# Attention with compressed, selected and local keys: two heads side by side on 64-row tiles, and the compressed keys of four tiles and two heads as one unit

## The chip, the core and the metric

The kernel runs on one core of one Trainium2 chip. The metric is device microseconds for one execution. TensorE (PE) does the matrix products, VectorE (DVE) and ScalarE (ACT) the elementwise work, GpSimd (POOL) some fills, and SyncE (SP) issues most transfers. Everything here is in 4-byte floats.

## The reference

Two transformer blocks run one after the other on 512 tokens of width 1024. The change is in the mixer of the second block, in the attention of its first eight heads. Each query head has 64 dimensions; four query heads share one of two key and value heads. Every query looks at three sets of keys, each with a softmax of its own, and the three results are added with one gate each:

```python
m_c = cmp_end[None, :] <= tpos[:, None]
s_c = jnp.einsum('bkgqd,bknd->bkgqn', qq, k_cmp) * scale      # 31 compressed keys
p_c = masked_softmax(s_c, m_c) * m_c
o_c = jnp.einsum('bkgqn,bknd->bkgqd', p_c.astype(v_cmp.dtype), v_cmp)
...                                                            # o_s: keys of selected blocks
...                                                            # o_w: keys of a local window
return gg[..., 0:1] * o_c + gg[..., 1:2] * o_s + gg[..., 2:3] * o_w
```

With 512 tokens there are 8 blocks of 64 keys and 16 may be selected, and the window is 512 long: selected and local keys are both all causal keys, each with its own keys and values. The second eight heads ("forgetting" attention) add a term from cumulated forget gates to the logits and are not in the change, though they run through one of the functions that it touches.

## The kernel before

Each engine has its own instruction stream, written as a list of phases; semaphores order the engines against each other. Tokens come in four tiles of 128. The eight heads are handled as four pairs: pair i holds one head of each key head, so a 128-partition column of queries holds two heads in rows 0 to 63 and 64 to 127. Four banks of PSUM take logits, two take turned probabilities, two take sums. The order of tiles is (2, 3, 1, 0), so a unit of tile q is q + 1 key blocks of 128 wide.

`grouped_attention` (L2422) goes through `attend` (L1498). For each pair a loop turn has 24 units: 2 heads, 4 tiles, 3 key sets. The compressed set is one unit of 128 columns (31 keys and padding) per head and tile. `copy_queries` (L2412) first copies each head's queries to a buffer whose other 64 rows are zero, so each logits product uses all 128 rows and a single head. A unit goes through: logits on PE (L1546); mask and row minimum on DVE (L1587); exponential with row sum on ACT (L1566); reciprocal (L1592) and a diagonal matrix with reciprocal times gate (L1597) on DVE; then PE multiplies each block of the probabilities with that diagonal, which turns and scales it in one (L1545); ACT copies the result out (L1571); PE sums with the values (L1553). The turn ends with ACT's copy of the pair's sums (L1575). At its start the turn waits for the work of the turn before.

`paired_attention` (L1610) is used for the first block's attention (name `dsa`) and for the forgetting attention (`fox`). It is written out without a loop. A unit is two heads of one tile. The logits of head 0 come from rows 0 to 63 and those of head 1 from rows 64 to 127 of the array (L1649), into two banks. DVE masks both heads (L1727), ACT takes both exponentials (L1698), DVE scales the probabilities in place (L1741, L1744), PE turns them with transposes (L1671), ACT copies both heads at once (L1708), and PE sums head 0 into columns 0 to 63 and head 1 into columns 64 to 127 (L1684). In step t the engines take these up in this order:

```python
# PE:  logits(t), turn(t - 2), sums(t - 3)
# ACT: exponentials(t), copy(t - 2)
# DVE: mask and minimum(t), scaling(t - 1)
```

turn(n) waits for scaling(n) and copy(n - 1), sums(n) for copy(n), logits(t) for the masking of unit t - 2. `fox` units have one more product per head, from the forget sums (L1652). `dsa` pairs also make their keys and values on the way (L2004 to L2020).

Of the kernel before, what the change touches and what calls it, by code (L numbers as in the profile page):

```python
# [23 lines left out]
NCMP = 31  # L24
CMP_L = 32
# [9 lines left out]
def columns(*parts):  # L35

    at, out = 0, {}
    for name, width in parts:
# [10 lines left out]
CB = columns(("causal", T), ("cos", T), ("sin", T), ("rot", P), ("twice0", P), ("twice1", P), ("cmp_mask", QT * P),  # L49
             ("cmp_valid", QT))  # L50
# [50 lines left out]
def build(nc, d):  # L101

    ctx = ExitStack()
    with ctx:
# [1393 lines left out]
        def attend(name, scope, turns, work, out, ready, before, zero_first=()):  # L1498


            N = len(work)
            sx = keep(f"{name}_masked", [P, 4, T], scope)
            probs = keep(f"{name}_probs", [P, 4, T], scope)
            probsT = keep(f"{name}_probsT", [P, 2, T], scope)
            diag = keep(f"{name}_diag", [P, 4, P], scope)
            stat = keep(f"{name}_stat", [P, 3, 4], scope)
            MAX, SUM, INV = range(3)
            L, TR, O = 0, 4, 6
            order = []
            for t in range(N + 4):  # L1510
                order += [("L", t)] * (t < N) + [("T", t - 3)] * (3 <= t < N + 3) + [("O", t - 4)] * (t >= 4)
            a_order = []
            for t in range(N + 3):
                a_order += [("exp", t)] * (t < N) + [("PT", t - 3)] * (t >= 3)
            d_order = []
            for t in range(N + 1):
                d_order += [("max", t)] * (t < N) + [("inv", t - 1), ("diag", t - 1)] * (t >= 1)

            def names(eng, seq):
                return before[eng][0] + [f"{a}{n}" for a, n in seq]  # L1520
            S = {"pe": steps(f"{name}_pe", names("pe", order)), "act": steps(f"{name}_act", names("act", a_order) + ["out"]),
                 "dve": steps(f"{name}_dve", names("dve", d_order))}

            def earlier(what, n, back, turn):

                who = S[{"max": "dve", "T": "pe", "PT": "act", "O": "pe"}[what]]
                return who(f"{what}{n - back}", turn) if n >= back else who(f"{what}{N + n - back}", turn, 1)

            def pe(pe):
                S["pe"].enter(pe)  # L1530
                for r in ready:
                    pe.wait_ge(*reached(*r))
                with pe.Fori(0, turns) as i:
                    before["pe"][1](pe, i, S)
                    for what, n in order:
                        w = work[n]
                        if what == "L":
                            pe.wait_ge(*earlier("max", n, 4, i))
                            out_l = ps[:, L + n % 4, 0:w["w"]]
                            ins = mm(out_l, w["query"], w["keys"])  # L1540
                        elif what == "T":
                            pe.wait_ge(*S["dve"](f"diag{n}", i))
                            pe.wait_ge(*earlier("PT", n, 2, i))
                            for b in range(w["w"] // P):
                                ins = mm(ps[:, TR + n % 2, b * P:(b + 1) * P], probs[:, n % 4, b * P:(b + 1) * P], diag[:, n % 4, :])  # L1545
                        else:  # L1546
                            pe.wait_ge(*S["act"](f"PT{n}", i))
                            if n == 0:
                                pe.wait_ge(*S["act"]("out", i, 1))
                            hh, q = w["head"], w["tile"]  # L1550
                            nb = w["w"] // P
                            for b in range(nb):
                                ins = mm(ps[hh * HD:(hh + 1) * HD, O, q * P:(q + 1) * P], w["values"][b],  # L1553
                                         probsT[:, n % 2, b * P:(b + 1) * P], w["first"] and b == 0, w["last"] and b == nb - 1)
                        ins.then_inc(*S["pe"].step(f"{what}{n}"))

            def act(act):
                S["act"].enter(act)
                with act.Fori(0, turns) as i:
                    before["act"][1](act, i, S)  # L1560
                    for what, n in a_order:
                        w = work[n]["w"]
                        if what == "exp":
                            act.wait_ge(*S["dve"](f"max{n}", i))
                            act.wait_ge(*earlier("T", n, 4, i))
                            ins = nc.scalar.activation(probs[:, n % 4, 0:w], sx[:, n % 4, 0:w], ACT.Exp, scale=-1.0,  # L1566
                                                       bias=stat[:, MAX, n % 4:n % 4 + 1], accum_out=stat[:, SUM, n % 4:n % 4 + 1])
                        else:
# [487 lines left out]
        def mixer_inputs(scope, h, branch):  # L2056
# [54 lines left out]
            def pool(pool):  # L2111
                pool.wait_ge(*reached(*branch[0]))
                for n in (kcmp, vcmp):
                    nc.gpsimd.memset(n[:, :], 0.0).then_inc(zeroed, 1)
# [827 lines left out]
```

## Time and profile before

| | |
|---|---|
| median of 3 runs | 3237.2 us (3234.42 to 3240.36) |
| the profiled execution | 3233.23 us |
| its span in the profile | 3231.4 us |
| the changed attention, from the last head input to the first product of `fox` | 2477.1 to 2657.5 us |
| `fox`, four pairs | 2657.5 to 2705.9 us |

The span is from the first to the last instruction. Times inside the profile are microseconds from its start. PE, DVE and ACT shares of a window say how busy an engine was; "PEld" is the load of the array's stationary operand, which overlaps products. A 4-byte product shows as two records, a transpose as one. PEclk is the granted clock of TensorE as a share of 2.4 GHz.

### The profile page before, as it was taken

Reading aid. Unit: us, or ns where it says so; the run is one execution under the profiler, and the core shown is the slowest. Engines: PE = TensorE matmul, PEld = TensorE weight load, DVE = VectorE, ACT = ScalarE, POOL = GpSimd, SP = SyncE. Lnnn points to the kernel's source line nnn. Section 1 sums busy time; section 2 is a strip of 40 time slices with the busy share of each in tenths; the row PEclk is TensorE's granted clock in tenths of the full one; section 3 lists DMA queues with packets and bytes.
Section 4 is the critical chain, followed back from the end, with each engine's and each line's share of the span. In section 5 each row is a group of like instructions: output and inputs, shape, how many; then the busy total and the mean of one; then the engine's idle time right before and its main releaser. Section 6 shows DMA issues by size and latency. Waiting matters only on the chain.

```text
span 3231.4 us, 49675 instructions
## 1 busy us (share of the span) xinstructions
PE 2942.0 (91%) x19222; PEld 2146.1 (66%) x19222; DVE 1448.2 (45%) x2408; ACT 1060.4 (33%) x1648; POOL 231.5 (7%) x221
## 2 busy tenths in 40 slices
PE   4998999888999899879999799999898997899998
PEld 1566666637888644558888488886655665688885
DVE  6466555624333327654333443332335555533335
ACT  1323222214432222634431344311112555344214
POOL 1122222201000101300000000000001000000000
PEclk9999999999999989999999899999798998999999
DMA  4223222222222111022222123221120000222312
GB/s 185 89 90 112 103 103 102 94 104 78 104 96 108 61 40 65 1 78 80 102 101 107 40 78 104 101 98 68 54 83 33 1 0 14 91 104 91 115 54 98
DMA packets 45837, 260.85 MB, mean 81 GB/s; under 512 B 4952, under 2 KB 7400, under 8 KB 26888
## 3 DMA queue, kind: packets, MB, share of 16 engines
q1 hardware_dynamic: 45128, 254.33, 22.2%
q10 hardware_dynamic: 576, 4.57, 0.4%
q8 instruction: 105, 1.72, 0.2%
q14 instruction: 28, 0.23, 0.0%
HBM read 256.73 MB, written 2.15 MB: 80 GB/s over the span
## 4 chain that ended last, share of the span: by engine, by line
PE 83%; DVE 7%; issue 3%; ACT 3%; DMA 2%; POOL 1%; PEld 1%; DVEq 0%; SPq 0%; ACTq 0%; POOLq 0%; PEldq 0%
PE psum L191 82%; DMA weights<-in_ada 1%; DVE weights L227 1%; PEld psum L191 1%; PE psum L1671 1%; DVE ln_rstd L1134 0%; DVE attention_in L1727 0%; POOL join L507 0%; POOL join L496 0%; POOL XT_pairs L500 0%; ACT dsa_probs L1698 0%; DVE rms_rstd L1214 0%; DVE dsa_probs L1744 0%; DVE group_norm L765 0%; DVE ff_weights_lo L1246 0%
## 5 line engine op out<-in xcount | busy, mean ns | idle before, releaser
L1246 DVE TENSOR_TENSOR ff_weights_lo<-weights,ff_weights_hi 128x1024 fp32r<-128x1024 f32 (+1 forms) x120 | 159.7, 1332 | 328.6 <-ACT ff_weights_hi L1243 328.6
L1246 DVE TENSOR_TENSOR ffn_weights_lo<-weights,ffn_weights_hi 128x1024 fp32r<-128x1024 f32 (+1 forms) x120 | 159.7, 1332 | 322.0 <-ACT ffn_weights_hi L1243 322.0
L191 PE MATMUL psum<-ff_in_hi,ff_weights_hi 128*128 128x512 f32 x704 | 276.2, 392 | 21.0 <-DVE ff_in_lo L1143 17.6
L191 PE MATMUL psum<-ffn_in_hi,ffn_weights_hi 128*128 128x512 f32 x704 | 276.0, 392 | 17.9 <-DVE ffn_in_lo L1222 14.4
L1243 ACT ACTIVATE ffn_weights_hi<-weights 128x1024 fp32r<-128x1024 f32 (+1 forms) x120 | 137.4, 1147 | 448.1 <-PE psum L191 448.1
L1243 ACT ACTIVATE ff_weights_hi<-weights 128x1024 fp32r<-128x1024 f32 (+1 forms) x120 | 137.4, 1147 | 445.1 <-PE psum L191 445.1
L191 PE MATMUL psum<-ffn_in_lo,ffn_weights_hi 128*128 128x512 f32 x704 | 275.5, 391 | 0.0
L191 PE MATMUL psum<-ff_in_hi,ff_weights_lo 128*128 128x512 f32 x704 | 275.4, 391 | 0.0
L191 PE MATMUL psum<-ff_in_lo,ff_weights_hi 128*128 128x512 f32 x704 | 275.3, 391 | 0.0
L191 PE MATMUL psum<-ffn_in_hi,ffn_weights_lo 128*128 128x512 f32 x704 | 275.1, 391 | 0.0
L191 PEld LDWEIGHTS psum<-ff_in_hi,ff_weights_hi 128*128 128x128 f32 x704 | 133.2, 189 | 51.4 <-issue 19.2
L191 PEld LDWEIGHTS psum<-ffn_in_hi,ffn_weights_hi 128*128 128x128 f32 x704 | 133.1, 189 | 48.3 <-issue 16.0
L191 PEld LDWEIGHTS psum<-ffn_in_hi,ffn_weights_lo 128*128 128x128 f32 x704 | 133.1, 189 | 27.8
L191 PEld LDWEIGHTS psum<-ff_in_lo,ff_weights_hi 128*128 128x128 f32 x704 | 133.3, 189 | 27.6
L191 PEld LDWEIGHTS psum<-ff_in_hi,ff_weights_lo 128*128 128x128 f32 x704 | 133.0, 189 | 27.9
L191 PEld LDWEIGHTS psum<-ffn_in_lo,ffn_weights_hi 128*128 128x128 f32 x704 | 133.1, 189 | 27.5
L191 PE MATMUL psum<-ff_hidden_hi,ff_weights_hi 128*128 128x512 f32 x352 | 136.9, 389 | 0.0
L191 PE MATMUL psum<-ff_hidden_lo,ff_weights_hi 128*128 128x512 f32 x352 | 136.9, 389 | 0.0
L191 PE MATMUL psum<-ffn_hidden_hi,ffn_weights_hi 128*128 128x512 f32 x352 | 136.9, 389 | 0.0
L191 PE MATMUL psum<-ffn_hidden_lo,ffn_weights_hi 128*128 128x512 f32 x352 | 136.9, 389 | 0.0
L191 PE MATMUL psum<-ff_hidden_hi,ff_weights_lo 128*128 128x512 f32 x352 | 136.9, 389 | 0.0
L191 PE MATMUL psum<-ffn_hidden_hi,ffn_weights_lo 128*128 128x512 f32 x352 | 136.9, 389 | 0.0
(452 smaller groups left out, 5383.4 us busy)
## 6 DMA issues: line engine op xcount, KB each, us to landing
weights<-in_ada SPq DMA_DIRECT2D x96, 512.0 KB, 4.3
weights<-in_ff_in SPq DMA_DIRECT2D x44, 1024.0 KB, 4.7
weights<-in_ffn_in SPq DMA_DIRECT2D x44, 1024.0 KB, 4.7
weights<-in_ff_out SPq DMA_DIRECT2D x16, 1408.0 KB, 6.0
weights<-in_ffn_out SPq DMA_DIRECT2D x16, 1408.0 KB, 6.0
weights<-in_rwkv SPq DMA_DIRECT2D x8, 1792.0 KB, 8.0
weights<-in_fox_qkv SPq DMA_DIRECT2D x4, 1536.0 KB, 6.7
residual<-in_x ACTq DMA_DIRECT2D x2, 2048.0 KB, 10.7
```

Source lines behind the costliest of these rows:

```text
L191: return nc.tensor.matmul(out, lhsT, rhs, start=start, stop=stop)
L227: return nc.vector.tensor_tensor_reduce(ada_tile(n), ada_tile(n), cond, scale=1.0, scalar=0.0, op0=ALU.mult, op1=ALU.add, accum_out=inner[ ...
L1243: return nc.scalar.activation(sp_.hi[u][:, 0:width], slot[s][:, u * width:(u + 1) * width], ACT.Copy)
L1246: return nc.vector.tensor_tensor(sp_.lo[u][:, 0:width], slot[s][:, u * width:(u + 1) * width], sp_.hi[u][:, 0:width].bitcast(F32), ALU.sub ...
L1671: ins = nc.tensor.transpose(ps[:, TR + hh, blk], probs[:, n % 3, hh, blk], ident)
```

## The change

`attend` and `pair_queries` are removed. `grouped_attention` now builds units for `paired_attention`: per pair eight units of two heads (four tiles, selected and local keys) and one "blocks" unit that holds the compressed keys of all four tiles and both heads in 256 columns, 32 for each tile and head. The compressed values of the two key heads lie in partitions 0 to 30 and 32 to 62 now, in their own columns. Gates go into the scaling of the probabilities. The sums of tile q start with the compressed part, then selected, then local keys. The fill of zeros around the queries and their copies go; the mask table of the compressed keys shrinks from 512 to 256 columns. `fox` now waits for the first of two conditions only, which is the last copy of sums.

```diff
-        def attend(name, scope, turns, work, out, ready, before, zero_first=()):
...
+                        if "blocks" in u:
+                            for q in range(QT):
+                                for hh in range(2):
+                                    ins = mm(ps[:, 2 * (t % 2) + hh, q * NB:(q + 1) * NB], u["query"][hh][:, q * P:(q + 1) * P], u["keys"][hh])
+                        for hh in range(0 if "blocks" in u else 2):
                             ins = mm(ps[:, 2 * (t % 2) + hh, 0:u["w"]], u["query"][hh], u["keys"][hh], True, "extra" not in u)
...
+                        if "blocks" in units[n]:
+                            for q in range(QT):
+                                ins = mm(ps[0:2 * NB, TR, q * P:(q + 1) * P], probs[:, n % 3, 0, q * 2 * NB:(q + 1) * 2 * NB], ident)
...
+                        if "blocks_at" in u:
+                            q = u["blocks_at"]
+                            for hh in range(2):
+                                rows = slice(hh * NB, (hh + 1) * NB)
+                                ins = mm(ps[hh * HD:(hh + 1) * HD, O + u["pair"] % 2, q * P:(q + 1) * P], small.values[rows, hh * HD:(hh + 1) * HD],
+                                         small.probsT[rows, u["pair"] % 2, q * P:(q + 1) * P], True, False)
...
+                        if "blocks" in units[t]:
+                            act.wait_ge(masked, 2 * (n0 + t) + 2)
+                            nc.scalar.activation(probs[:, t % 3, 0, 0:w], sx[:, t % 2, 0, 0:w], ACT.Exp, scale=-1.0).then_inc(exped, 2)
...
+                        if "blocks" in units[n]:
+                            nc.scalar.activation(small.probsT[:, units[n]["pair"] % 2, :], ps[0:2 * NB, TR, :], ACT.Copy).then_inc(copied, 1)
...
+                            nc.vector.tensor_tensor(by_tile, ps[:, 2 * (t % 2):2 * (t % 2) + 2, 0:QT * NB].rearrange("p h (q n) -> p q h n", n=NB),
+                                                    u["mask"].rearrange("p (q h n) -> p q h n", q=QT, h=2), ALU.add).then_inc(small.sem, 1)
+                            dve.wait_ge(small.sem, done + 1)
+                            nc.vector.tensor_reduce(least, by_head, AX.X, ALU.min).then_inc(small.sem, 1)
+                            dve.wait_ge(small.sem, done + 2)
+                            nc.vector.tensor_tensor(by_head, by_head, least.unsqueeze(2).to_broadcast([P, 2 * QT, NB]),
+                                                    ALU.subtract).then_inc(masked, 2)
...
+                            nc.vector.tensor_reduce(small.total, by_head, AX.X, ALU.add).then_inc(small.sem, 1)
+                            dve.wait_ge(small.sem, done + 3)
+                            nc.vector.reciprocal(small.share, small.total).then_inc(inverted, 1)
+                            dve.wait_ge(inverted, n0 + n + 1)
+                            nc.vector.tensor_tensor(small.share.rearrange("p (q h) -> p q h", h=2), small.share.rearrange("p (q h) -> p q h", h=2),
+                                                    units[n]["gate"], ALU.mult).then_inc(small.sem, 1)
+                            dve.wait_ge(small.sem, done + 4)
+                            nc.vector.tensor_tensor(by_head, by_head, small.share.unsqueeze(2).to_broadcast([P, 2 * QT, NB]),
+                                                    ALU.mult).then_inc(scaled, 2)
...
+                            gate = units[n]["gate"][hh] if "gate" in units[n] else None
+                            nc.vector.tensor_scalar(probs[:, n % 3, hh, 0:w], probs[:, n % 3, hh, 0:w], stat[:, n % 4, INV, hh:hh + 1], gate,
+                                                    ALU.mult, ALU.bypass if gate is None else ALU.mult).then_inc(scaled, 1)
...
-                        last = mm(ps[0:NCMP, 6, g * HD:(g + 1) * HD], hidden[:, 1, m, g * NCMP:(g + 1) * NCMP],
+                        last = mm(ps[g * NB:g * NB + NCMP, 6, g * HD:(g + 1) * HD], hidden[:, 1, m, g * NCMP:(g + 1) * NCMP],
...
-                a(vcmp[0:NCMP, :], ps[0:NCMP, 6, 0:P], ACT.Copy).then_inc(*act_done.step("v2"))
+                for g in range(2):
+                    rows, cols = slice(g * NB, g * NB + NCMP), slice(g * HD, (g + 1) * HD)
+                    ins = a(vcmp[rows, cols], ps[rows, 6, cols], ACT.Copy)
+                ins.then_inc(*act_done.step("v2"))
...
+            for i in range(N):
+                units.append({"pair": i, "w": 2 * QT * NB, "query": [queries[r, i, :] for r in halves],
+                              "keys": [t["keys_cmp"][r, 0:NB] for r in halves], "mask": cc("cmp_mask"), "blocks": True, "blocks_at": STEP_TILES[0],
...
+                for q in STEP_TILES:
...
+                    for b, (keys, v0) in enumerate(((t["keys_slc"], 0), (t["keys_win"], P))):
...
+                        own = {"blocks_at": q} if b == 0 and q != STEP_TILES[0] else {}
...
+                nc.vector.tensor_scalar(of_blocks, of_blocks, cc("cmp_valid"), None, ALU.mult).then_inc(valid_done, 1)
+                dve.wait_ge(valid_done, 1)
```

## Rows read from the trace of the kernel before

**Rows 1.** The page: span, busy time of PE, and the chain that ended last.

```profile
span 3231.4 us, 49675 instructions
...
PE 2942.0 (91%) x19222; PEld 2146.1 (66%) x19222; DVE 1448.2 (45%) x2408; ACT 1060.4 (33%) x1648; POOL 231.5 (7%) x221
...
PE 83%; DVE 7%; issue 3%; ACT 3%; DMA 2%; POOL 1%; PEld 1%; DVEq 0%; SPq 0%; ACTq 0%; POOLq 0%; PEldq 0%
```

**Rows 2.** Windows: stretch, length, busy PE, PEld, DVE, ACT, POOL, clock, DMA.

```profile
2477.10:2482.20 5.10, 0.00 (x0) 0.00 (x0) 3.75 (x3) 0.00 (x0) 5.04 (x4) 0.50 0.00 0
2482.20:2528.70 46.50, 43.97 (x241) 31.76 (x241) 24.88 (x104) 22.39 (x73) 7.03 (x4) 0.90 0.07 25
2528.70:2571.40 42.70, 40.29 (x241) 29.54 (x241) 21.85 (x101) 22.98 (x74) 0.00 (x0) 1.00 0.00 0
...
2657.50:2705.90 48.40, 42.71 (x368) 27.66 (x368) 26.38 (x112) 31.04 (x85) 0.00 (x0) 1.00 0.00 1
```

**Rows 3.** Windows: a steady pair of `fox`, one of `dsa`, the compressing products.

```profile
2668.67:2680.17 11.50, 10.75 (x95) 6.80 (x93) 6.58 (x28) 7.67 (x21) 0.00 (x0) 1.00 0.01 2
...
1309.60:1322.55 12.95, 10.55 (x90) 6.74 (x88) 9.08 (x30) 8.21 (x23) 5.28 (x8) 1.00 0.00 0
...
2310.00:2340.00 30.00, 27.43 (x128) 27.38 (x128) 5.91 (x10) 2.25 (x4) 0.00 (x0) 0.50 0.21 72
```

**Rows 4.** Groups by form, 2477 to 2657.5 us: busy us, mean ns, idle before.

```profile
L191 PE MATMUL psum<-nsa_diag,nsa_probs 128*128 128x128 f32 x384 | 61.0, 282 | 6.8 <-DVE nsa_diag L1597 5.0 <-DVE nsa_stat L1592 1.8
...
L191 PE MATMUL psum<-nsa_probsT,values 128*64 128x128 f32 x320 | 48.6, 283 | 2.5 <-ACT nsa_probsT L1571 1.4
L1597 DVE TENSOR_SCALAR nsa_diag<-const_all,nsa_stat,pair_gates 128x128 f32<-128x128 f32 x96 | 35.2, 367 | 12.3 <-DVE nsa_stat L1592 0.4
```

**Rows 5.** Groups by form, 2657.5 to 2706 us (`fox`).

```profile
L191 PE MATMUL psum<-fox_probsT,heads_fox_v 128*64 128x128 f32 x160 | 12.2, 283 | 0.0
L1671 PE MATMUL psum<-const_all,fox_probs 128*128 128x128 f32 x80 | 12.0, 281 | 4.9 <-ACT fox_probsT L1708 3.5 <-DVE fox_probs L1744 1.4
...
L1708 ACT ACTIVATE fox_probsT<-psum 128x768 f32<-128x768 f32 x4 | 3.2, 806 | 0.0
...
L1744 DVE TENSOR_SCALAR fox_probs<-fox_probs,fox_stat 128x128 f32<-128x128 f32 x8 | 1.9, 284 | 0.1
```

**Rows 6.** Timeline of `fox`: start, length, instruction, idle time before.

```profile
2678.66 0.30 PEld L191 LDWEIGHTS psum<-heads_fox_k,heads_fox_q 64*128 64x128 f32 x4 [0.17 <-issue]
2678.66 0.92 PE L191 MATMUL psum<-heads_fox_k,heads_fox_q 64*128 64x384 f32 x4
...
2679.41 0.81 PE L191 MATMUL psum<-forget_right,forget_left 64*128 64x384 f32 x4
...
2680.27 0.56 DVE L1727 CUSTOM_DVE_ANT_0 fox_masked<-psum,const_attention 128x384 f32<-128x384 f32 x1 [2.10 <-PE psum L191]
2680.73 0.85 PEld L191 LDWEIGHTS psum<-fox_probsT,heads_fox_v 128*64 128x64 f32 x16 [0.17 <-issue]
...
2680.93 0.62 ACT L1698 ACTIVATE fox_probs<-fox_masked,fox_stat 128x384 f32<-128x384 f32 x1 [1.82 <-DVE fox_stat L1727]
...
2681.54 0.60 ACT L1698 ACTIVATE fox_probs<-fox_masked,fox_stat 128x384 f32<-128x384 f32 x1
2681.76 0.30 PEld L191 LDWEIGHTS psum<-heads_fox_k,heads_fox_q 64*128 64x128 f32 x4 [0.17 <-issue]
...
2682.14 0.57 ACT L1708 ACTIVATE fox_probsT<-psum 128x512 f32<-128x512 f32 x1
```

**Rows 7.** Groups: the nearest rows for the blocks unit (2300 to 2345 us; whole span).

```profile
L191 PE MATMUL psum<-cmp_blocks,weights 128*128 128x62 f32 x128 | 27.5, 421 | 7.6 <-DVE keys_sin L2260 7.6
...
L736 DVE TENSOR_TENSOR Nab_pairs<-psum,const_recurrence 128x256 f32<-128x256 f32 x8 | 3.3, 413 | 0.0
```

**Rows 8.** Timeline at the start of the changed attention.

```profile
2477.10 0.95 POOL L2410 MEMSET nsa_queries<- 128x1024 f32 x1 [247.12 <-DVE heads_fox_k L2378]
...
2478.39 3.70 DVE L2418 COPY nsa_queries<-heads_nsa_q 64x512 f32 x2 [1.35 <-POOL nsa_queries L2410]
```

More of the change, by code:

```diff
@@ L1608, in build, with paired_attention @@
         paired_so_far = [0, 0]
-        def paired_attention(name, scope, units, out, ready, made=None, masks_made=None, over=None):
+        def paired_attention(name, scope, units, out, ready, made=None, masks_made=None, over=None, small=None):
             N = len(units)
@@ L2026, in sparse_attention @@
                     w = (q + 1) * P
-                    units.append({"pair": i, "tile": q, "w": w, "query": [qs[r, i, q * P:(q + 1) * P] for r in halves],
+                    units.append({"pair": i, "tile": q, "w": w, "first": True, "last": True, "query": [qs[r, i, q * P:(q + 1) * P] for r in halves],
                                   "keys": [made_keys[r, i % 3, 0:w] for r in halves], "mask": [own_mask[q][:, hh, :] for hh in range(2)],
@@ L2112, in pool @@
                 pool.wait_ge(*reached(*branch[0]))
[L2113 to L2114 removed]
+                nc.gpsimd.memset(kcmp[:, :], 0.0).then_inc(zeroed, 1)
+                nc.gpsimd.memset(vcmp[:, :], 0.0).then_inc(zeroed, 1)
                 nc.gpsimd.memset(z[:, 4, :], 1.0).then_inc(zeroed, 1)
@@ L2399, in head_inputs @@
             return out, [(dve_done, "fk", N - 1), (act_done, "fk std", N - 1)]
-        def pair_queries(name, scope, source, ready):
-            qz = keep(f"{name}_queries", [P, 2, T], scope)
-            zeroed = sem(f"{name}_queries_zeroed")
-            def pool(pool):
-                for r in ready:
-                    pool.wait_ge(*reached(*r))
-                nc.gpsimd.memset(qz[:, :, :], 0.0).then_inc(zeroed, 1)
-            def copies(dve, i, S, last):
-                dve.wait_ge(zeroed, 1)
-                dve.wait_ge(*S["pe"](last, i, 1))
-                alone(dve)
-                for hh in range(2):
-                    r = slice(hh * HD, (hh + 1) * HD)
-                    nc.vector.tensor_copy(qz[r, hh, :], tile_of(source, i)[r, :]).then_inc(*S["dve"].step(f"q{hh}"))
-            return qz, pool, copies
@@ L2490, in forgetting_attention @@
                     tok = slice(q * P, (q + 1) * P)
-                    units.append({"pair": i, "tile": q, "w": w, "query": [heads["fox_q"][r, i, tok] for r in halves],
+                    units.append({"pair": i, "tile": q, "w": w, "first": True, "last": True, "query": [heads["fox_q"][r, i, tok] for r in halves],
                                   "keys": [heads["fox_k"][r, i, 0:w] for r in halves], "mask": [cc("causal")[:, T - w:T]] * 2,
```

211 lines of the change are left out of this document (60 added, 151 removed).

## The prediction, made before the changed kernel ran

> **What bounds the kernel now.** The page comes first [rows 1]: PE is busy 91% of the span and makes up 83% of the chain that ended last, so the question is how long PE is held in the stretch that changes. The windows [rows 2] cut that stretch. The changed attention lies between 2477.1 us, when the last head input is written, and 2657.5 us, when `fox` gets its first product: 180.4 us. 5.1 us of it are a wait without PE, 46.5 us the first pair, 42.7 us each of the next two, and the rest (43.4 us) the last pair with its way out. In a steady pair PE is busy 40.29 of 42.70 us, DVE and ACT about half. What replaces these units has to be read from the two stretches that run `paired_attention` already. A steady pair of `fox` (four units of two heads) takes 11.50 us with PE busy 10.75, one of `dsa` 12.95 with PE busy 10.55, both at clock 1.00 [rows 3].
>
> Why PE holds the old stretch so long shows in the groups [rows 4, 5]. The 384 products with the diagonal keep PE busy 61.0 us, 159 ns a record; the 80 transposes of `fox` 12.0 us, 150 ns a record, and a block takes one such record where it took two. The 320 value products of one head take 152 ns a record, the 160 of `fox`, two heads in the two column halves, 76 ns. So two things halve: the turning per block, and the value sums per record. The logits do as well: four records of 384 columns, two heads, in 0.75 us, from 2678.66 to 2679.41, where the next product starts [rows 6].
>
> **The change, part by part.** All sums are from 2477.1 us to the first product of `fox`.
>
> *The start.* The fill, the copies and the wait go: PE had to wait for POOL's fill and two copies that took 3.70 us [rows 7]. Now its first product waits for the last head input alone: 5.1 us gone [rows 2]. The DVE multiplication of gates with the valid column comes first on DVE instead, one small instruction beside PE's first logits: nothing, 0.3 us without that cover.
>
> *The two-head units, 32 of them, eight to a pair.* PE's own work per unit, with n key blocks: 16 value records are loaded in 0.85 us [rows 6], 53 ns each, and there are 4n, 0.213n us; the turning takes 2n records of about 107 ns, 0.213n, and the logits 0.213n. Each of the three groups starts 0.17 us late (marked "issue") [rows 6], 0.5 us a unit. That is 0.5 + 0.64n; over two sets of n = 1 to 4 it is 4.0 + 12.8 = 16.8 us a pair. This is a floor, not the forecast. Without the second product of `fox` a dependence is longer than PE's work. Turn(t) waits for copy(t - 1), which is behind the exponentials of t + 1 in ACT's queue, which wait for the masking and so for logits(t + 1). From logits(t + 1) with n = 3 [rows 6]: 0.92 to the end of the product and 0.05 to DVE (the 0.05 is from 2680.22, the end of the second product, to 2680.27), 0.66 to the first exponential (2680.27 to 2680.93), 0.61 and 0.60 for the two (2680.93, 2681.54, 2682.14), 0.81 for the copy of 768 columns [rows 5], 0.13 to PE. That is 3.78 us. Then come turn(t) and sums(t - 1), 0.81 and 0.80 with their gaps, before logits(t + 3). So two units take 5.39 us, one 2.70. Of this 1.2 us goes with n (six terms of about 0.2 a block, the mask 0.13 and copies and exponentials 0.21 each), so a unit takes 0.9 + 0.6n: 1.5, 2.1, 2.7, 3.3, together 9.6 for one set and 19.2 us a pair of heads. Checked on what exists: `fox` adds its second product once per two units, 10 blocks x 0.213 / 2 = 1.1, giving 10.7 against 11.50 measured; `dsa` adds about 2.2 for making keys and values, 11.8 against 12.95 [rows 3]. The steps between unlike sizes cost the missing 0.8 us in `fox`. The new pair has as many changes of size with twice the units: 19.2 + 0.8 = 20.0 us.
>
> *The gates* ride on the scaling as a second scalar. A 128x128 operation with two scalars took 367 ns (L1597), one with one scalar 284 [rows 4, 5]: 0.08 us x 64 = 5 us on DVE, which in the loop above is beside ACT (DVE's scaling ends before ACT's exponentials of the next unit). Nothing; 5 us if DVE were on the path.
>
> *The blocks unit, four of them.* Its logits are 16 records, its turning 8, its value sums 16 over the pair. No row shows a 32-column product on 64 rows. Records of 62 columns took 27.5 us for 128, 0.215 each, at clock 0.50 [rows 8, 3]; at full clock half, 0.107, no less than 128 columns take, so loads set the pace and short columns save nothing. Side by side it is 53 ns: 0.85 us for the logits, 1.7 if the heads did not overlap, and I take the first, as the rows of the 64-row products are the nearest. Turning 8 x 0.107 = 0.85, sums 16 x 0.053 = 0.85 (1.7 if not side by side), gaps 0.5: 3.0 us of PE. On DVE it is seven instructions in a row that wait for each other; the 256-wide ones are near 413 ns [rows 8], five of those and two small ones are some 2.5 us, against 2.2 for a usual unit. ACT has less than usual. Between 3 us (PE) and 6 us (the whole chain of it uncovered) I take 3.0, since its DVE work overlaps the neighbours' PE work: 12 us for four. The 32 compressed units of the old form, with 64 records of logits, 64 of values, and a sixth of the products with the diagonal, are inside the 180.4.
>
> *Filling and emptying.* `fox` took 48.4 us for four pairs of 11.50: 2.4 us over [rows 2, 3]. The first pair before took 46.5 instead of 42.7 us, with the clock at 0.90 after the wait and POOL at work: 3.8 us, kept, since PE still idles 5 us before the stretch (0.50 in the window before) [rows 2] and POOL still fills the forget sides then.
>
> *The rest.* Two small ACT copies in place of one in the inputs of the mixer, a shorter table, one condition less before `fox` (PE's own sums, done before ACT's copy of them): nothing, at most 0.3 us.
>
> Sum: 4 x (20.0 + 3.0) + 2.4 + 3.8 = 98.2 us instead of 180.4. 82.2 us less than the profiled execution's 3233.2 makes 3151. The median of the runs shown is 4.0 us above that execution, 3155 by it. I say 3153 us, between the two. What follows is a chain through `fox`'s start to the output projection, whose weights were brought long before, so the saving is handed on whole.
>
> A rule speaks against the change: the Trainium skill, "TensorEngine Tiling (Array Packing)", Key Properties, says that changing the tiling mode drains TensorE. The new unit changes shape three times (64 rows, full, 64 columns). The page gives no figure; the timeline shows 0.17 us at such a step [rows 6], which the sum has. By the rule alone more switches would cost more, yet the old units switched twice each in 96 units (192 times) and the new ones thrice in 36 (108): by the count 84 x 0.17 = 14 us are saved, not lost. That is inside the two stretches compared.
>
> **The rivals.**
> 1. *PE's work sets the pace.* If ACT's copy is early enough, a pair takes 16.8 + 3.0 = 19.8: 79 + 2.4, and perhaps 2 for the cold start, 84 us, 3137. For it: PE was busy 10.75 of 11.50 in `fox`. Against: `fox` has 2.1 us more PE work a pair to cover with, and `dsa` is at 10.55 of 12.95. Chance 0.14.
> 2. *The chain of DVE and ACT is longer.* `dsa`'s pace without its 2.2 is 2.69 us a unit: 86 us for 32, blocks units at 6 us 24, with 6.2 it is 116: 3169. For it: dependent DVE operations on small data and the second scalar. Against: `dsa` has POOL's masks beside DVE, absent here. Chance 0.27.
> 3. *It doesn't do what it says:* heads don't overlap in the new shapes, so logits and sums take 0.43n each: 25.4 a pair and 4.6 for blocks, 126 us, 3179. Against: the `fox` records. Chance 0.04.
> 4. *Slower:* a PE that waits oftener keeps its half clock. At 1.2 GHz throughout, a pair is about 38 us, the stretch 160, and `fox` 37 longer: 3250. It decides if the half clock covers more than some 85% of both. Against: `dsa` at clock 1.00 with PE busy 81% [rows 3]. Chance 0.02.
>
> **How the numbers follow.** The forecast (0.52) has a range of its own of 3145 to 3161. The range 3138 to 3176 leaves out most of rival 1's low end and all beyond rival 2. About 0.2% (6 us) is what a measurement of this kernel can tell from no change. Faster by more: all but rival 4 and 0.01 for something unseen, 0.97; same 0.01; slower 0.02.
>
> **What would show it.** The stretch from the last head input to `fox`'s first product 98 us long, first product near 2477.3; a steady pair near 23 us; PE busy some 85% of it at clock 1.00; transposes x160 plus 32 records for the blocks; before L1671 PE's idle time released by ACT's copy. If DVE is the releaser, or the step around a blocks unit takes over 4 us, rival 2 is right; PE over 95%, rival 1. A clock of 0.5 past 2490 us, or two heads' records one after the other, would make it wrong.

## The result, and the profile after

3154.89 us, the median of four runs (3152.18 to 3157.25), against 3235.81 us of the kernel before on the same chip (3232.59 to 3240.36, four runs): ratio 0.9749, interval 0.9732 to 0.9766, so 81 us less. The forecast was 3153 us, from a stretch of 98.2 us. The profiled execution took 3152.2 us. (In the prediction the groups 7 and 8 are named the other way round: the start is in [rows 8], the nearest rows for the blocks unit are in [rows 7].)

From the page of the kernel after, which answers to [rows 1]:

```profile
span 3150.4 us, 47831 instructions
...
PE 2866.1 (91%) x19030; PEld 2082.4 (66%) x19030; DVE 1427.0 (45%) x2257; ACT 1033.0 (33%) x1526; POOL 230.3 (7%) x220
```

The shares don't show the change: PE is busy 91% of the span as before, with 76 us less work. The windows of the kernel after, with the columns of [rows 2]: the start until shortly after POOL is done, and a steady pair.

```profile
2477.65:2491.35 13.70, 10.39 (x48) 5.93 (x48) 11.70 (x24) 5.36 (x12) 10.75 (x6) 0.53 0.01 1
2504.53:2527.04 22.51, 20.67 (x194) 13.45 (x193) 16.62 (x63) 15.69 (x44) 0.00 (x0) 1.00 0.01 1
```

The last head input is done at 2477.62 us and `fox` gets its first product at 2575.65: 98.0 us where it was 180.4. Everything else stands where it stood (last head input at 2477.1 before; `fox` 48.45 us against 48.4). The blocks units' logits start at 2504.53, 2527.04 and 2549.55, so a pair takes 22.51 us. The first pair takes 26.9 us, 4.4 over, and the last with its way out 26.1, 3.6 over.

What PE waits for in that steady pair (waits of 2504.53 to 2527.04: who waits for whom, us in total, times, longest):

```profile
PEld psum L1571 <- DVE nsa_probs L1680: 3.7, 3, 1.5
PEld psum L192 <- issue: 3.4, 20, 0.2
...
PE psum L1571 <- ACT nsa_probsT L1620: 1.5, 3, 0.7
PEld psum L1571 <- issue: 1.0, 2, 0.5
PEld psum L192 <- DVE nsa_probs L1673: 0.7, 1, 0.7
```

L1571 is the transpose, L1607 the exponentials, L1620 the copy, L1680 the scaling. PEld and PE wait for the same turn, and the view puts one wait down to DVE's scaling and the other to ACT's copy. In the code both conditions stand ahead of the first load, so the later one counts. The timeline of the longest of these waits shows which it was:

```profile
2513.93 0.87 DVE L1680 TENSOR_SCALAR nsa_probs<-nsa_probs,nsa_stat,gates 128x384 f32<-128x384 f32 x2
...
2514.72 0.79 ACT L1620 ACTIVATE nsa_probsT<-psum 128x768 f32<-128x768 f32 x1
...
2515.62 0.64 PEld L1571 LDWEIGHTS psum<-const_all,nsa_probs 128*128 128x128 f32 x6 [1.54 <-DVE nsa_probs L1680]
```

The scaling is done at 2514.80, the copy at 2515.51, 0.11 us before the load. The other three turns that PE waits for look the same: the copy ends 0.11 us before the load, the scaling 0.1 to 0.6 us before the copy. So in the changed kernel ACT's copy holds PE at all four, and the scaling that the view names for PEld had been done before it.

The groups of the stretch after, in the form of [rows 4]:

```profile
L192 PE MATMUL psum<-nsa_probsT,values 128*64 128x128 f32 x320 | 24.8, 282 | 0.0
L1571 PE MATMUL psum<-const_all,nsa_probs 128*128 128x128 f32 x160 | 24.2, 282 | 6.6 <-ACT nsa_probsT L1620 5.5 <-ACT compressed_probsT L1618 0.6 <-DVE nsa_probs L1680 0.4
...
L192 PE MATMUL psum<-compressed_probsT,values_cmp 32*64 32x128 f32 x64 | 7.0, 293 | 0.0
...
L192 PE MATMUL psum<-const_all,nsa_probs 128*64 128x128 f32 x32 | 5.2, 316 | 1.8 <-DVE nsa_probs L1673 1.6
L192 PE MATMUL psum<-keys_cmp,heads_nsa_q 64*128 64x32 f32 x64 | 5.2, 306 | 5.2 <-DVE heads_fox_k L2317 5.2
...
L1680 DVE TENSOR_SCALAR nsa_probs<-nsa_probs,nsa_stat,gates 128x128 f32<-128x128 f32 x16 | 4.8, 343 | 0.3
...
L2385 DVE TENSOR_SCALAR gates<-gates,const_attention 128x8 f32<-128x8 f32 x1 | 3.6, 3606 | 0.0
```

The 384 products with the diagonal in 61.0 us have become 160 transposes in 24.2 and 32 records for the blocks units in 5.2, and the value sums, 320 records in 48.6 us when each came alone, are 320 in 24.8 side by side. Two things in it were not forecast: a second scalar costs 59 ns (343 against 284), not 83; and one DVE operation on eight columns took 3.6 us.

### The profile page after: what moved, and what is told of

It is laid out like the page before. It is cut to its first block, busy times and chain, and to the rows that moved or that the text cites. A ratio compares the mean times of both kernels' runs of the same rounds, so it can differ in the third digit from the quotient of the medians.

```text
span 3150.4 us, 47831 instructions
## 1 busy us (share of the span) xinstructions
PE 2866.1 (91%) x19030; PEld 2082.4 (66%) x19030; DVE 1427.0 (45%) x2257; ACT 1033.0 (33%) x1526; POOL 230.3 (7%) x220
## 4 chain that ended last, share of the span: by engine, by line
PE 83%; DVE 7%; ACT 3%; issue 3%; DMA 2%; POOL 1%; PEld 1%; DVEq 0%; SPq 0%; POOLq 0%; ACTq 0%; PEldq 0%
PE psum L192 81%; PE psum L1571 1%; DMA weights<-in_ada 1%; PEld psum L192 1%; DVE weights L228 1%; DVE ln_rstd L1135 0%; DVE attention_in L1650 0%; ACT nsa_probs L1607 0%; POOL join L508 0%; POOL join L497 0%; POOL XT_pairs L501 0%; DVE rms_rstd L1215 0%; DVE dsa_probs L1680 0%; DVE group_norm L766 0%; DVE ff_weights_lo L1247 0%
## 5 line engine op out<-in xcount | busy, mean ns | idle before, releaser
L192 PE MATMUL psum<-ffn_in_hi,ffn_weights_hi 128*128 128x512 f32 x704 | 275.9, 392 | 17.6 <-DVE ffn_in_lo L1223 14.2
```

Of the source, the lines that this page charges most:

```text
L192: return nc.tensor.matmul(out, lhsT, rhs, start=start, stop=stop)
```

## The experiments

Theory A is the forecast's account: a loop through DVE, ACT's exponentials and ACT's copy paces the units, and PE's work is nearly as long. The rivals were PE's own work alone, a longer DVE chain, and heads that don't overlap. Two lengths are compared throughout: the pair (from one blocks unit's logits to the next, equal to 0.02 us in both steady pairs of a run) and the stretch (last head input to `fox`'s first product). What lies ahead of the stretch shifts by up to 7 us from one trace to another, so single times are not compared below that. Runs 2 to 7, 9 and 10 have one execution each: 3169.9, 3159.5, 3157.3, 3140.3, 3171.8, 3157.6, 3151.0 and 3144.5 us.

The stretch also holds the moment at which PE's clock rises in the first pair, and that differs from trace to trace. Worked out from the mean clock of short windows, as under run 7, it comes 12.8 us after the first product in the changed kernel, 11.5 to 12.1 us in runs 1 to 4 and 9 to 11, 15.1 in runs 5 and 8, 16.0 in run 6 and 19.4 in run 7. The length of a steady pair is free of it, so where pair and stretch disagree, the pair is the surer one.

**1. ACT's copy first.** In the changed attention ACT takes copy(t - 2) before the exponentials of t.

```diff
-                    (exponentials of unit t)
                     (keys and values, if made here)
                     (copy of unit t - 2)
+                    (exponentials of unit t)
```

> Edit: in the new attention alone, ACT takes copy(t - 2) before the exponentials of unit t, not after them. In the changed kernel a steady pair takes 22.50 us and the stretch from the last head input to the first product of fox 98.0 us. Theory A (the loop from logits over mask, exponentials, ACT's copy and the turning is what sets the pace): the copy is no longer behind the exponentials, PE's own work of 19.8 us a pair comes next, a pair takes 20 to 21 us, the stretch about 8 us less. Theory B (PE's own work sets the pace already): no change, within 1 us. Theory C (DVE's queue sets the pace): no change or slower, since the exponentials, which DVE's scaling waits for, come later.

3148.35 us (3146.71 to 3150.95), ratio 0.9717, interval 0.9701 to 0.9733. A pair takes 21.55 us, 0.96 less, the stretch 93.9. The waits of a steady pair of this kernel (2505.81 to 2527.36); L1621 is the copy here, L1689 the scaling:

```profile
ACT nsa_probsT L1621 <- PE psum L1571: 3.8, 7, 1.0
PEld psum L192 <- issue: 3.4, 20, 0.2
PEld psum L1571 <- DVE nsa_probs L1689: 3.2, 4, 1.0
...
PE psum L1571 <- DVE nsa_probs L1689: 0.6, 2, 0.4
```

The copy no longer releases PE; it waits for PE now, and PE waits for DVE's scaling. So the dependence that the forecast named is real and worth 1 us of a pair and 4.1 of the stretch, half of the 8 that Theory A expected of this edit; Theories B and C, with no change, are out. PE is busy 20.68 of the 21.55 us that are left.

**2. Turn by products.** The 160 transposes become products with the unit matrix, two records each.

```diff
-                                ins = nc.tensor.transpose(ps[:, TR + hh, blk], probs[:, n % 3, hh, blk], ident)
+                                ins = mm(ps[:, TR + hh, blk], probs[:, n % 3, hh, blk], ident)
```

> Edit: the new attention turns its probabilities with products by the identity (two records a block) and not with transposes (one); fox and dsa are left. 40 more records of 107 ns a pair, 4.3 us of PE work. Theory A: the loop gave PE some slack, so a pair grows from 22.5 to about 24.4 us, the stretch by 7 to 8 us. Theory B: all of it shows, 4.3 us a pair, 17 us. Theory C: 0 to 4 us.

A pair takes 26.34 us, the stretch 112.7, the run 3169.9. A steady pair, windows:

```profile
2511.88:2538.22 26.34, 25.44 (x234) 18.75 (x232) 16.67 (x63) 15.91 (x43) 0.00 (x0) 1.00 0.01 2
```

PE's busy time grows by 4.8 us and 3.8 of them show. The loop of the forecast has one turn for two units, so by the loop alone some 2.4 would show, and Theory A expected 1.9. The result lies nearer to Theory B's 4.3: only 1 us was hidden in waits, and PE's own work counts for more of the pace than the forecast says.

**3. One head after the other.** The value sums take all blocks of head 0, then all of head 1.

```diff
-                        for b in range(0 if "blocks" in u else nb):
-                            for hh in range(2):
+                        order = [(b, hh) for hh in range(2) for b in range(nb)]
+                        for b, hh in ([] if "blocks" in u else order):
```

> Edit: the value sums of the new attention take all blocks of head 0 and then all of head 1, where they alternated. Nothing else changes, and the work is the same. If two heads overlap in the array only when their records alternate, the 80 records a pair cost 107 ns each in place of 53, 4.3 us more PE work a pair: by theory A 7 to 8 us on the stretch, by theory B 17 us. If the array overlaps them at any distance, no change. 16 value records are loaded in 0.85 us now; in the first case it is 1.7 us.

A pair takes 23.76 us, the stretch 102.8. Timeline of this kernel, one group of 12 value records:

```profile
2518.18 0.90 PEld L192 LDWEIGHTS psum<-nsa_probsT,values 128*64 128x64 f32 x12 [0.17 <-issue]
...
2519.25 0.30 PEld L192 LDWEIGHTS psum<-keys_slc,heads_nsa_q 64*128 64x128 f32 x4 [0.17 <-issue]
```

The loads of 12 records take 0.90 us here and 0.64 in the changed kernel, and the next group starts after 1.07 instead of 0.81 us. Twelve loads one behind the other would be 1.28 us, an estimate from the 107 ns a record of the transposes' loads. So alternating is worth 1.25 us a pair, where 0 or 4.3 were expected: heads that come in turn lose part of the overlap and keep part of it.

**4. No gates.** The scaling leaves out the gates of selected and local keys.

```diff
-                            gate = units[n]["gate"][hh] if "gate" in units[n] else None
+                            gate = None
```

> Edit: the scaling of the two-head units leaves out the gate of selected and local keys, so it has one scalar operand and not two (the gate of the compressed part stays). The output lacks these gates. The scaling of 128 columns took 343 ns with two and 284 with one. Theory A and B: DVE gains 0.06 us x 16 a pair and nothing is faster, stretch within 1 us. Theory C: 1 us a pair, 4 us on the stretch.

A pair takes 22.43 us, 0.08 less, the stretch 97.8; DVE is busy 15.67 instead of 16.62 us of a pair. 3.8 us of DVE work are free, as forecast.

**5. No blocks unit.** The four blocks units and their value sums are left out.

```diff
-                units.append({"pair": i, "w": 2 * QT * NB, ... "blocks": True, "blocks_at": STEP_TILES[0],
```

> Leaves the compressed part out: four pairs of eight two-head units and no blocks unit, so the output lacks the compressed keys' share. Theory A (the forecast): the blocks unit costs 3.0 us a pair, so a pair falls from 22.5 to 19.5 and the stretch from 98.0 to 86 us. Theory B (its DVE chain is uncovered): 6 us a pair, to 16.5, the stretch to 74. Theory C, from the counted records of the trace (16 loads in 0.97, turning 0.85, four value groups of 0.19 with a step of 0.17 each, and the steps before the first two groups): 3.6 us a pair, 18.9, the stretch 83.6.

A pair takes 19.37 us, 3.14 less, the stretch 86.7, the run 3140.3. Windows of a steady pair:

```profile
2506.00:2525.37 19.37, 17.23 (x156) 10.85 (x154) 14.27 (x57) 14.67 (x43) 0.00 (x0) 1.00 0.01 2
```

The blocks unit costs 3.1 us, on the forecast's 3.0; Theory C's 3.6 is too much and B's 6 out. PE's work falls by 3.44 us, so 0.3 of it had filled waits. (The stretch falls by 11.3 us and not by four times 3.14; in its first pair the clock rose 2.3 us later.) Without the unit the loop is easier to see: PE is idle 2.1 of 19.4 us, all of it put down to ACT's copy.

**6. Small units.** The compressed keys are a two-head unit of 128 columns for each tile.

```diff
-                    for b, (keys, v0) in enumerate(((t["keys_slc"], 0), (t["keys_win"], P))):
+                    for b, (keys, v0) in enumerate(((t["keys_cmp"], None), (t["keys_slc"], 0), (t["keys_win"], P))):
```

> The blocks unit undone: the compressed keys are one 128-column two-head unit for each tile again, still two heads side by side. Theory A: each such unit takes 0.9 + 0.6 = 1.5 us, four of them 6.0 in place of the blocks unit's 3.0: a pair of 25.5, the stretch 110. Theory B (PE's own work sets the pace, 0.5 + 0.64 a unit, 4.6 in place of some 3.6): a pair of 23.5, the stretch 102. Theory C (the blocks unit's DVE chain costs as much as the four small units save): no change within 0.3 us a pair.

A pair takes 25.56 us, the stretch 112.2, the run 3171.8. Windows of a steady pair:

```profile
2514.21:2539.77 25.56, 22.06 (x194) 13.63 (x192) 18.92 (x86) 19.39 (x62) 0.00 (x0) 1.00 0.00 1
```

Against the pair without compressed keys that is 6.2 us for four units, 1.55 each where Theory A had 1.5. PE's work would have allowed 4.8. This is the clearest sign of the loop: units of one block cost what the loop says and not PE's work, and PE idles 3.5 us of the pair, in eight waits that the view puts down to ACT's copy. The single unit for four tiles is worth 3.05 us a pair, 12.2 in all; of the 14.2 between the stretches (112.2 less 98.0) the rest lies in the first pair, where the clock rose 3.2 us later, and in the way out.

**7. The multiplication with the valid column early.** It moves from the start of this attention to the end of DVE's phase before.

```diff
-                nc.vector.tensor_scalar(of_blocks, of_blocks, cc("cmp_valid"), None, ALU.mult).then_inc(valid_done, 1)
...
+                dve.wait_ge(*act_done("gates"))
+                ts(of_blocks, of_blocks, cc("cmp_valid"), None, ALU.mult).then_inc(valid_done, 1)
```

> The multiplication of the compressed gates with the valid column is moved from the first place on DVE in this attention to the end of DVE's phase before. Theory A (DVE's 3.61 us at the start held up the first mask, and with it the whole attention): the first mask starts some 1.7 us earlier and the stretch falls from 98.0 to about 96.3. Theory B (the start is held by PE's half clock and its own work anyway): no change of the stretch beyond 0.3 us. Pairs stay at 22.5 us in both.

The first mask starts 2.06 us after the first logits instead of 3.62. Yet the stretch is 99.9 us, 1.9 longer: both theories wrong. Two things differ in the first pair, DVE's scaling and PE's clock. The scaling in the changed kernel (timeline):

```profile
2477.65 3.61 DVE L2385 TENSOR_SCALAR gates<-gates,const_attention 128x8 f32<-128x8 f32 x1
...
2479.42 1.81 POOL L2403 MEMSET forget_right<- 128x2048 f32 x1
...
2481.29 0.42 DVE L1640 TENSOR_TENSOR nsa_masked<-psum,const_attention 128x256 f32<-128x256 f32 x1
...
2486.84 1.80 POOL L2407 MEMSET forget_right<- 1x2048 f32 x1
2486.98 2.27 DVE L1680 TENSOR_SCALAR nsa_probs<-nsa_probs,nsa_stat,gates 128x384 f32<-128x384 f32 x2
```

and with the multiplication early:

```profile
2489.36 1.80 POOL L2407 MEMSET forget_left<- 1x2048 f32 x1
2489.60 0.16 DVE L1676 RECIPROCAL nsa_stat<-nsa_stat 128x2 f32<-128x2 f32 x1
2489.80 3.53 DVE L1680 TENSOR_SCALAR nsa_probs<-nsa_probs,nsa_stat,gates 128x384 f32<-128x384 f32 x2
...
2491.22 1.90 POOL L2408 MEMSET forget_right<- 1x2048 f32 x1
```

The eight-column operation ends at 2481.26, 0.03 us after POOL's second fill (2481.23); the two scalings that take 0.87 us later in the run end 0.6 us after a fill (2488.64) in one kernel and 0.2 after one (2493.12) in the other. Masks, minima and reciprocals run beside fills at their usual length in both. The start of the kernel before, which [rows 8] show in part, has one more such operation, a copy of 24 columns, and one that goes through:

```profile
2481.87 1.96 POOL L2477 MEMSET forget_left<- 1x2048 f32 x1
2482.12 1.75 DVE L2448 COPY pair_gates<-gates 128x24 f32 x1
...
2483.89 1.79 POOL L2478 MEMSET forget_right<- 1x2048 f32 x1
2483.91 0.33 DVE L2453 TENSOR_SCALAR pair_gates<-pair_gates,const_attention 128x1 f32<-128x1 f32 x2
```

The copy ends 0.04 us after a fill; two multiplications of a single column take 0.33 us together in the midst of the next one. So a DVE copy or a multiplication with scalars waited until POOL's fill was over in all these rows but the single-column one. In the changed kernel the scaling was released just behind the start of the last of the six fills and waited for that one; with the mask early it was released during the fifth and waited for two.

The other thing is PE's clock. Windows of 3 us, first of the changed kernel, then of this one:

```profile
2489.67:2492.67 3.00, 2.77 (x16) 1.40 (x14) 2.44 (x8) 1.88 (x5) 0.00 (x0) 0.87 0.13 34
```

```profile
2500.05:2503.05 3.00, 3.00 (x26) 1.89 (x24) 1.33 (x7) 1.41 (x4) 0.00 (x0) 0.76 0.04 14
```

All windows of the first pair before these are at 0.50, all behind at 1.00. A mean of 0.87 means 0.8 us at 0.50, so the full clock (2.4 GHz) came 12.8 us after the first product at 2477.67; here by the same way 1.4 us into the window, 19.4 us after 2482.05.

It is the clock that cost the time, not the longer scaling. The first transposes of the changed kernel, then of this one:

```profile
2489.87 1.14 PE L1571 MATMUL psum<-const_all,nsa_probs 128*128 128x128 f32 x6
```

```profile
2493.39 1.54 PE L1571 MATMUL psum<-const_all,nsa_probs 128*128 128x128 f32 x6 [0.63 <-DVE nsa_probs L1680]
```

They start 12.20 us after the first product there and 11.34 here, so the early multiplication did put PE 0.86 us ahead. From them to the second pair's logits it is 14.66 us there and 17.34 here, 2.7 longer, with the clock at 0.50 for the first 8.1 us here and for 0.6 there.

A rule of the Trainium skill bears on this ("SBUF — State Buffer", Who interferes with whom): GpSimd shares a pair of SBUF ports with VectorE, `copy` and `tensor_scalar` can take that pair, when their operands meet conditions that the page names, and who comes first holds it for its whole instruction. These rows agree, with ends 0.03, 0.6 and 0.2 us after a fill's; run 9 tests it. By the same rule the copies of 3.70 us in [rows 8] were waits for POOL too, which no run tried.

**8. Copy first in all three attentions, and the multiplication early.**

```diff
-                    copy_first = name == "nsa"
+                    copy_first = True
```

> ACT takes the copy of the turned probabilities before the exponentials of the next unit in all three attentions that run through this function, and the multiplication with the valid column is early. Theory A: the two savings in the changed stretch add up, 4.1 us by the run with the copy first and 0 to 1.7 by the early multiplication, and the forgetting attention (11.50 us a pair) and the first block's (12.95) gain at most what the copy held there: 3.5 of the 4.9 us of idle time before the transposes of the forgetting attention, so 2 to 3.5 us, and as much in the first block's. In all 8 to 12 us, ratio near 0.969 to the kernel before. Theory B (outside the changed stretch the copy first makes DVE or the exponentials late by as much): only the 4 to 6 us, ratio near 0.971. Theory C: with two units of exponentials later, the other two attentions become slower and the whole is no better than the changed kernel, 0.975.

3147.99 us (3143.51 to 3154.34), ratio 0.9729, interval 0.9715 to 0.9743. The stretch is 95.0 us, 1.1 more than with the copy first alone. As in run 7 the first transposes come earlier, by 0.6 us, and the clock rises later, 15.1 us after the first product instead of 11.7. Steady pairs of `dsa` and `fox`, windows, beside [rows 3]:

```profile
1296.30:1309.01 12.71, 10.59 (x88) 6.77 (x87) 9.02 (x30) 8.23 (x23) 5.28 (x8) 1.00 0.01 1
2580.01:2591.04 11.03, 10.78 (x94) 6.80 (x92) 6.67 (x28) 7.54 (x22) 0.00 (x0) 1.00 0.01 1
```

`dsa` gains 0.24 us a pair, `fox` 0.47, about 2 us each over all their pairs. With the 3.0 of the stretch that is 7 us by the traces, where Theory A expected 8 to 12. The times don't show even this: the ratio is above the 0.969 of Theory A and the 0.971 of Theory B, and its interval overlaps that of run 1 and that of the changed kernel.

**9. The sides by transfers.** On the changed kernel, POOL's six fills are replaced by eight transfers from a table in memory.

```diff
-                for n in (left, right):
-                    nc.gpsimd.memset(n[:, :, :], 0.0).then_inc(zeroed, 1)
...
+                for n, side in enumerate((left, right)):
+                    for i in range(4):
+                        sp.dma_start(side[:, i, :], d["forget_sides"][n, :, :]).then_inc(zeroed, 16)
```

> The changed kernel with one edit: POOL's six fills of the forget sides, 10.75 us from the last head input on, are replaced by eight transfers of a table of zeros and ones from memory. POOL then does nothing while the attention starts. Theory A (a DVE operation with one source and scalars can't start while POOL's fill runs): the 8-column multiplication falls from 3.61 to about 0.2 us, the first two 384-column scalings from 2.27 us for two to 0.87, the first mask follows the first logits after 2.1 instead of 3.6 us, and the stretch falls by 2 to 4 us, from 98.0 to 94 to 96. Theory B (these times are the first use of DVE's operation or of its tables, and POOL has nothing to do with it): both stay long, the stretch stays at 98. Theory C (the start is bound by PE at its half clock): they get short and the stretch stays at 98.

Timeline of this kernel:

```profile
2476.54 0.23 DVE L2385 TENSOR_SCALAR gates<-gates,const_attention 128x8 f32<-128x8 f32 x1
...
2478.60 0.42 DVE L1640 TENSOR_TENSOR nsa_masked<-psum,const_attention 128x256 f32<-128x256 f32 x1 [1.82 <-PE psum L192]
...
2484.29 0.87 DVE L1680 TENSOR_SCALAR nsa_probs<-nsa_probs,nsa_stat,gates 128x384 f32<-128x384 f32 x2
```

3.61 became 0.23 us, 2.27 became 0.87: it was POOL. The stretch is 96.6 us, 1.4 less, between Theory A's 2 to 4 and Theory C's nothing. Of the 1.6 us gained at the first mask and the 1.4 at the scaling half is not seen: PE's clock is at 0.50 for 11.6 of these microseconds (12.8 before), and PE's own work fills more of them: the first transposes come 1.6 us earlier and directly behind the logits.

Behind the stretch the gain is lost again in this trace. `fox`, from its first product to the end of its last copy, takes 51.2 us against 48.3 in the changed kernel, because PE's clock falls in it. PE was busy 5.7 of the 7.4 us from 2573.1 to 2580.5, as much as in the same part of the changed kernel, where the clock stayed. Then, windows:

```profile
2580.50:2587.00 6.50, 6.11 (x28) 3.90 (x28) 0.91 (x7) 2.04 (x6) 0.00 (x0) 0.50 0.00 0
```

The clock falls in `fox` in runs 3, 6 and 10 too (1.4 to 1.6 us longer); why it fell in these four and not in the others is open. A shorter stretch is therefore not yet a shorter run.

**10. Copy first, early multiplication, sides by transfers.**

> The kernel with ACT's copy first and the early multiplication, and the sides by transfers as well. Theory A (POOL's fills held the first scaling for 3.5 us there): 0.87 us for the two scalings, and 1.5 to 3 us less than the 95.0 us of the stretch without this edit. Theory B: no change, 95.0.

The stretch is 93.1 us, 1.9 less than in run 8, inside the 1.5 to 3 expected. The scalings take 0.87 us, pairs 21.55. Not all of the 1.9 is the scalings' doing: the first transposes come 0.7 us earlier, and the clock rises 11.7 us after the first product instead of 15.1.

**11. The same, and the exponential's table early.**

```diff
+                    phase(act=lambda act: nc.scalar.activation(warm[:, :], const("rms_eps"), ACT.Exp))
```

> As the run before, and the exponential's table is called for by one exponential of one column at the end of ACT's head inputs, before the attention starts. Theory A (the 1.28 us of the table load lie on the path of the first exponential): another 0.5 to 1.3 us off the stretch, in all 91 to 93 us, and a time near 3142 us, ratio 0.970 to the kernel before. Theory B (the stretch's start is bound by PE's half clock): the table load is hidden, no change to the run before.

3147.37 us (3142.17 to 3148.99), ratio 0.9706, interval 0.9693 to 0.9719; the stretch is 92.6 us, inside the 91 to 93 expected, while the time is 5 us above the 3142 expected (the kernel before took 3240.8 us beside it, 5 above the 3235.8 beside the changed kernel). The table load (1.28 us) moved to 4.4 us before the first product, and 0.5 us came of it. Better than the changed kernel's 0.9749 beyond both intervals, and not told apart from run 1 (0.9717).

## Why the prediction was right

**The start.** Right that PE waits for the last head input alone: its first product is at 2477.67. Wrong that the multiplication costs "nothing": it held the first mask for 1.6 us, not by its own work but by POOL's fills, which [rows 8] already showed beside two copies of 3.70 us. The prediction took their length for granted instead of asking why 512 columns on 64 rows take so long. To take the multiplication away from there put PE 0.86 us ahead, and a later rise of the clock took more than that back (run 7). The sign "a clock of 0.5 past 2490 us" was just met: the full clock came at 2490.5.

**The two-head units.** 20.0 us a pair forecast, 19.37 measured (run 5). The loop is there: with the copy first the pair falls by 1 us, the small units take 1.55 us for the 1.5 of 0.9 + 0.6n, and ACT's copies are what ended PE's idle time before the transposes, 6.1 of 6.6 us. But it isn't the pace for all sizes. PE's own work was put at 16.8 us and is 17.2; with the blocks unit it is 20.7 of 22.5, 92% busy where 85% was forecast. Added work in the turning shows at 80% (3.8 of 4.8 us, run 2). Rival 1's 19.8 for the whole pair lacks 0.9 us of PE's work and the 1.8 of waits that are left. The timeline of the steady pair has these waits unit by unit: 0.60 us where ACT's copy stood behind the exponential of the blocks unit, 0.19 behind those of the second three-block unit, 0.74 and 0.17 behind those of the two four-block units, and none where it stood behind units of two blocks and one. Shown: both limits act, the loop there and PE's own work elsewhere. So "one unit takes 0.9 + 0.6n" is right as a sum over the sizes and not as the pace of each.

**The gates.** Nothing, shown by run 4; the price a unit was 0.12 us of DVE, not 0.16.

**The blocks unit.** 3.0 forecast, 3.1 measured. Inside it one term was off: the 16 value sums stand with four tiles, each a group of its own that starts 0.17 us late, 0.36 us a tile (from 2508.35 to 2508.71) and 1.44 in all where 0.85 and one step of 0.17 were forecast. The logits took 0.97 us for 16 records instead of 0.85, so the heads overlap. It came out right because the unit filled 0.3 us of waits. DVE's seven operations, five of them 0.41 to 0.43 us, were hidden for the most part: the first three hold the unit's exponential for 2.3 us, and the wait of 0.60 us behind it is theirs. Rival 2's 6 us is out.

**Filling, emptying and the cold start.** 2.4 + 3.8 = 6.2 us forecast, 4.4 + 3.6 = 8.0 measured. These 1.8 us are paid by the pairs, 22.51 instead of 23.0, four times 0.5. 98.0 against 98.2 is in part this luck: the parts are right to 2 us each.

**The steps between shapes.** The prediction counted 192 such steps in the old stretch and 108 in the new one, and 14 us saved by them. It doesn't hold: PEld's waits put down to "issue" are 4.3 us of a steady pair before and 4.4 us (3.4 and 1.0) after. The step of 0.17 us inside the sum is there, 20 times a pair, and the forecast doesn't rest on the count.

**The rivals.** Rival 1 and 2 each told a part: PE is 92% busy, and DVE's scaling holds PE once the copy comes first (run 1); neither's time came. Rival 3 is out by the 0.97 us of the logits and by run 3. Rival 4 is out for the changed kernel: clock 1.00 in the steady pair with PE 92% busy, and in `fox`. What is left open is why PE got its full clock after 11.5 us in one trace and 19.4 in another. More idle time is not the reason: before the rise PE was busy 17.1 of 19.4 us in run 7, 9.5 of 12.8 in the changed kernel and 8.4 of 11.7 in run 1. With one trace of each kernel it can't be said whether the moment belongs to the kernel or to the execution.

## What to carry to other kernels

Where a pipeline of four engines replaces one that was bound by PE, work out both PE's own work per unit and the longest loop through the engines' queues: here they were within 15% of each other, and an edit on either gives back only part of its worth (1 of 2 us, 3.8 of 4.8). Many small units of one step are the dear ones, since the loop has a fixed part (1.55 us for one block as measured, 0.6 for each more by the forecast's working); one unit for four tiles saved 12 us. An operation that is much longer than its size says is probably waiting for something: look at which engine's instruction ends with it before it is copied into a sum or moved, since moved it may meet the next one. Where the waits view names one engine for a wait on several conditions, compare the ends in the timeline: here the engine named had been done for up to 0.8 us. And look at the clock before a longer or shorter first pair is put down to an edit.

## What was unexpected of the hardware

- DVE's operations with one source (a copy, a multiplication with scalars) did not run beside a fill on POOL: 3.61 us for eight columns beside two fills of 1.81 us, 0.23 without them; 3.53 or 2.27 us for two scalings that take 0.87; 1.75 us for a copy of 24 columns (this one seen only beside a fill). Only multiplications of a single column went through, two in 0.33 us. Operations on two sources (L1645, 0.43 us with both in SBUF), reductions and reciprocals kept their length beside a fill. A fill of a single row, 1x2048, takes 1.80 us as one of 128 rows does, and holds DVE as long.
- Two heads in the two column halves overlap even when their records don't alternate: 12 records in 0.90 us in turn, 0.64 alternating, against some 1.28 without overlap (estimated from 107 ns a record).
- Products of 32 columns on 64 rows are no faster than value products of 128 columns: 16 in 0.97 us, 61 ns each against 53 (12 in 0.64), with PEld busy all of the 0.97.
- The clock can fall inside a stretch that other traces run at full clock: in run 9 `fox` has 6.5 us at 0.50 and takes 2.9 us longer.
